# Decay exponents of an SSD mixer: from pairs of matmuls in PSUM to running sums that return broadcast from DRAM

## The reference, cut to what matters

```python
a_cs = jnp.cumsum(d * a, axis=2)                  # per chunk; d > 0, a < 0
seg = a_cs[:, :, :, None] - a_cs[:, :, None, :]   # l, s
decay = jnp.exp(jnp.where(causal, seg, -jnp.inf))
cb = jnp.einsum('bclgn,bcsgn->bclsg', cc, bc)
y_diag = jnp.einsum('bclsgr,bcsgrp->bclgrp', cb[..., None] * decay, xdt)
```

## Time and profile before

| | us |
|---|---|
| median of 3 runs (2773.5 to 2775.04) | 2773.87 |
| span of the profiled execution, first to last instruction | 2771.6 |
| TensorE busy | 2748.3 (99%) |
| VectorE busy | 1604.5 (58%) |
| ScalarE busy | 1183.0 (43%) |
| GpSimd busy | 1096.0 (40%) |
| DMA queue of SyncE, share of the 16 engines' span | 50.4% |

### The profile page before, as it was taken

How to read it: one execution, slowest core, us unless ns; L and a number is a source line. 1 busy time by engine, 2 the same in 40 slices (tenths; PEclk the granted TensorE clock), 3 DMA queues, 4 the chain that set the end, 5 groups by cost and what they waited for, 6 DMA issues and landing times.

```text
span 2771.6 us, 35692 instructions
## 1 busy us (share of the span) xinstructions
PE 2748.3 (99%) x13342; PEld 2298.7 (83%) x13342; DVE 1604.5 (58%) x2236; ACT 1183.0 (43%) x2110; POOL 1096.0 (40%) x799
## 2 busy tenths in 40 slices
PE   8999999999999999999999999999999999999998
PEld 6788888888888888888888888888888888888887
DVE  4687623666426665147673466664444666666666
ACT  2465544455325554155542545554454332222223
POOL 1365541223101222002233578866555435353434
PEclk9999999999999999999999999999999999999999
DMA  9765486443456335554436456584344942333323
GB/s 293 242 216 193 159 295 236 183 169 136 183 197 228 122 122 190 188 207 176 150 121 241 163 178 243 197 300 164 134 162 146 361 157 92 124 134 123 128 92 152
DMA packets 215786, 505.65 MB, mean 182 GB/s; under 512 B 12970, under 2 KB 96558, under 8 KB 206142
## 3 DMA queue, kind: packets, MB, share of 16 engines
q1 hardware_dynamic: 215614, 503.37, 50.4%
HBM read 357.57 MB, written 145.75 MB: 182 GB/s over the span
## 4 chain that ended last, share of the span: by engine, by line
PE 97%; DVE 1%; issue 1%; DMA 1%; POOL 0%; ACT 0%; DVEq 0%; POOLq 0%; ACTq 0%
PE bank L2024 22%; PE bank L1692 21%; PE bank L1992 21%; PE bank L1736 13%; PE bank L1716 7%; PE bank L1827 3%; PE bank L1832 2%; PE bank L1811 1%; PE bank L1633 1%; PE bank L1794 1%; PE bank L1783 1%; PE bank L1817 1%; PE bank L1805 1%; PE bank L1755 1%; PE bank L1947 0%
## 5 line engine op out<-in xcount | busy, mean ns | idle before, releaser
L1692 PE MATMUL bank<-hnT_hi,w_ring 128*128 128x512 f32 x1152 | 374.7, 396 | 0.0
L2161 DVE SCALAR_TENSOR_TENSOR acc<-pre,par,acc 128x512 f32<-128x512 f32 x240 | 217.1, 904 | 108.0 <-ACT pre L1230 102.3
L2024 PE MATMUL bank<-w_first,T_hi 128*128 128x512 f32 x896 | 275.9, 389 | 0.9 <-issue 0.9
L1692 PEld LDWEIGHTS bank<-hnT_hi,w_ring 128*128 128x128 f32 x1152 | 216.4, 188 | 44.9 <-ACT win_tmp L1339 0.5
L1992 PE MATMUL bank<-T_hi,w_both 128*128 128x512 f32 x768 | 242.1, 389 | 0.2 <-DVE ff L2444 0.2
L1736 PE MATMUL bank<-w_ring,T_hi 128*128 128x512 f32 x768 | 241.9, 396 | 0.0
L2503 DVE TENSOR_TENSOR acc_th<-bank,acc_th 128x512 f32<-128x512 f32 x224 | 149.9, 686 | 153.9 <-PE bank L2024 153.7
L983 POOL TENSOR_TENSOR small<-small 128x1 f32<-128x1 f32 (+1 forms) x71 | 17.9, 252 | 528.8 <-ACT yo L1313 322.3
L1692 PE MATMUL bank<-hnT_lo,w_ring 128*128 128x512 f32 x576 | 224.4, 390 | 0.0
L2024 PEld LDWEIGHTS bank<-w_first,T_hi 128*128 128x128 f32 x896 | 168.1, 188 | 36.0 <-issue 1.2
L1716 PE MATMUL bank<-w_ring,hnT_hi 128*128 128x384 f32 x768 | 197.9, 338 | 0.0
(11 more groups left out here) (310 smaller groups left out, 6339.7 us busy)
## 6 DMA issues: line engine op xcount, KB each, us to landing
w_ring<-w_scr SPq DMA_DIRECT2D x312, 512.0 KB, 4.2
T_scr<-stage SPq DMA_DIRECT2D x32, 1792.0 KB, 6.5
w_scr<-w_both SPq DMA_DIRECT2D x104, 512.0 KB, 4.0
pair_raw<-in_w_ff SPq DMA_DIRECT2D x36, 1024.0 KB, 5.4
third<-T_scr SPq DMA_DIRECT2D x28, 1024.0 KB, 4.8
pair_raw<-T_scr SPq DMA_DIRECT2D x28, 1024.0 KB, 4.8
raw<-in_w_in SPq DMA_DIRECT2D x36, 512.0 KB, 5.5
w_raw<-in_w_ff SPq DMA_DIRECT2D x12, 1024.0 KB, 7.4
```

Of the source, the lines that this page charges most:

```text
L1692: mm = nc.tensor.matmul(bank[s][:, :], w[:, k, :], t[:, k, :], start=(k == 0 and j == 0), stop=(k == KT - 1 and j == 2))
L2024: mm = nc.tensor.matmul(bank[4 * half + t][:, :], a[:, k, tok], w[:, k, :], start=(SECOND[q % 7] not in GOES_ON and k == 0 and j == 0), st ...
L2161: ins = nc.vector.scalar_tensor_tensor(acc[:, s, 0:TB], pre[:, s, k:k + TB], w, acc[:, s, 0:TB], ALU.mult, ALU.add)
```

## The change

E is now made without matmuls. The copy `acsT` (24 rows) is stored in DRAM once a block, in four small DMAs (`store_sums`), and each step's 768 sums (one chunk, six heads) come back by a DMA that reads the same 3 KB for all 128 partitions (`load_sums`, 384 KB a step), into one of four slots of `sums`, one for each chunk. ScalarE computes Relu(acs[s] - sums[l]) with six operations, one for each head, since the bias `acs` is one number per partition and head; then Exp(-x), in the first block too. `acs` gets a place of its own. The matmuls L1778 and L1783, `running_sums`, `negated_sums`, the low part and their set-up go; VectorE masks C x B in the first block too. The slots of group 0 are loaded right behind the stores, those of later groups one by one, each behind the Exp that read the slot before.

```diff
@@ block.sync
+                def store_sums(b):
+
+                    acsT_ready.wait(sp, b, 1)
+                    for g in range(GROUPS):
+                        rows = slice(g * HEADS_PER_GROUP, (g + 1) * HEADS_PER_GROUP)
+                        sp.dma_start(sums_scr[b, g].rearrange("c (r l) -> r c l", l=P),
+                                     acsT[rows, :].rearrange("r (c l) -> r c l", l=P)
+                                     ).then_inc(sums_stored.sem, 16)
+
+                def load_sums(b, g, c):
+
+                    if g:
+                        exp_ready.wait(sp, b, (g - 1) * CH + c + 1)
+                    sp.dma_start(sums[:, c, :, :].rearrange("p r l -> p (r l)"),
+                                 sums_scr[b, g, c].partition_broadcast(P)
+                                 ).then_inc(sums_loaded[c].sem, 16)
...
                     for n in range(RING, U_OUT):
                         load(N0 + n, in_unit(n))
+                        if n == 11:
+                            store_sums(b)
+                            sums_stored.wait(sp, b, 16 * GROUPS)
+                            for c in range(CH):
+                                load_sums(b, 0, c)
+                        g, j = divmod(n, UNITS_G)
+                        if g >= 2 or g == 1 and j >= 5:
+                            after = {5: 0, 7: 1, (0 if b else 1): 2, 3: 3}.get(j)
+                            done = g if j >= 5 else g - 1
+                            if after is not None and 0 < done < GROUPS:
+                                load_sums(b, done, after)
                         if n == 11 and b:
                             hT_ready.wait(sp, b - 1, KT)
@@ block.scalar
                         if q == 0:
                             acsT_ps.wait(act, b, 1)
-                            nc.scalar.activation(acsT[0:HEADS, :], bank[3][0:HEADS, :], ACT.Copy
-                                                 ).then_inc(acsT_hi_ready.sem, 1)
-                            negated_sums(b, 0)
+                            nc.scalar.activation(acsT, bank[3][0:HEADS, :], ACT.Copy
+                                                 ).then_inc(acsT_ready.sem, 1)
...
-                        ab_ps.wait(act, b, q + 1)
+                        sums_loaded[c].wait(act, b, 16 * (g + 1))
                         ydiag_ps.wait(act, b, q)
-                        halves = E[:, :, :].rearrange("p (j r) l -> p j (r l)", j=2)
-                        if b == 0:
-                            nc.scalar.activation(halves, decay_ps[:, :, 0:GW], ACT.Exp
-                                                 ).then_inc(exp_ready.sem, 1)
...
-                        if c == 0 and g + 1 < GROUPS:
-                            negated_sums(b, g + 1)
+                        for r in range(HEADS_PER_GROUP):
+                            o = c * HEADS + g * HEADS_PER_GROUP + r
+                            fall = nc.scalar.activation(E[:, r, :], sums[:, c, r, :], ACT.Relu,
+                                                        scale=-1.0, bias=acs[:, o:o + 1])
+                        fall.then_inc(fall_ready.sem, 1)
+                        fall_ready.wait(act, b, q + 1)
+                        nc.scalar.activation(E[:, :, :], E[:, :, :], ACT.Exp, scale=-1.0
+                                             ).then_inc(exp_ready.sem, 1)
@@ block.tensor, slot1
                     if q == 0:
                         down_add.wait(pe, b, 0)
-                    if g == 0:
-                        seg_l_ready.wait(pe, b, c + 1)
-                    if c == 0:
-                        seg_s_ready.wait(pe, b, g + 1)
-                    exponent_read(b, q)
-                    if b == 0:
-                        for j in range(2):
-                            nc.tensor.matmul(
-                                bank[4 + j][:, 0:GW].rearrange("p (r l) -> p r l", l=P),
-                                ident_r[:, :], barred[:, :].unsqueeze(1).to_broadcast([P, 3, P]),
-                                start=True, stop=False)
-                    for j in range(2):
-                        mm = nc.tensor.matmul(
-                            bank[4 + j][:, 0:GW].rearrange("p (r l) -> p r l", l=P),
-                            seg_s[:, g % 2, cols], seg_l[:, c, 3 * j:3 * j + 3, :],
-                            start=b > 0, stop=True)
-                    mm.then_inc(ab_ps.sem, 1)
+                        acsT_ready.wait(pe, b, 1)
@@ block.vector
                         cb = bank[3][:, GW:GW + P]
-                        if b:
-                            steps.link(nc.vector.tensor_tensor(cb, cb, tri[:, :], ALU.mult))
+                        steps.link(nc.vector.tensor_tensor(cb, cb, tri[:, :], ALU.mult))
...
-                        if q < CH - 1:
-                            running_sums(b, q + 1)
```

89 lines of the change are left out of this document (14 added, 75 removed).

## The result

The change made the kernel slower, by 12 us where 0.5 us of gain was forecast.

The account below looks back on a forecast made before the run. TensorE, busy 99% of the span, was taken as the bound. The terms -31.4 + 2.3 + 1 + 13.2 + 14.4 = -0.5 us on a span of 2771.6 gave a median of 2773.4 us, range 2756 to 2789.

Parts of the forecast that it names:

- ScalarE's lateness: Mixer steps where TensorE waits for a later ScalarE: 2.3 us lost in the first block, 1 us in later ones.
- What goes from TensorE: Exponent matmuls removed from all mixer steps: 12.2 us gained in the first block, 19.2 in later ones, together 31.4.
- 0.05 us a step for L1832: Each mixer step: L1832, then followed by a float32 transpose, takes 0.65 us instead of 0.70.
- Later blocks' gain: Later blocks lose L1783 alone: 0.40 us a step, 19.2 us gained over 48 steps.
- ScalarE: Each step: six Relus end after 1.85 us, where one took 0.86; bounds 1.6 and 2.4.
- First block's queue: First block's start: sums' transfers on SyncE delay the splits' stores, stalling units 10 to 12; 13.2 us, bounds 8 and 19.
- Later blocks' queue: Later blocks' starts: sums fill the DMA queue, unit 15's weights land late; 4.8 us a block, 14.4 in three.
- Rival 1: Later blocks: the queue hides the broadcasts, a block loses 0.5 us instead of 4.8; 2760 us, chance 0.27.
- Rival 2: Block starts: TensorE's clock falls to half in stalls from about 3 us on; 2783 us, chance 0.17.
- Rival 3: Relus or broadcasts at their upper bounds: 7 to 16 us more, 2785; chance 0.14 together with Rival 4.
- Rival 4: SyncE's waits for the Exps also stall steps; little effect expected, chance 0.14 together with Rival 3.

Follow-up runs that it names:

- the kernel without trips: The changed kernel without the sums' stores, broadcasts and waits through DRAM, their tile filled with zeros once: 2759.05 us, ratio 0.9947.
- the best order: The changed kernel with SyncE's transfers (sums, h) reordered and y's transposes of steps 0 to 13 in PSUM bank 4: 2753.96 us, ratio 0.9926.
- h later: The changed kernel with the 2 MB load of h behind the load of unit 20 instead of unit 12: 2780.0 us, ratio 1.0023.

## Why the prediction was wrong

The forecast was 28.1 us of gain (31.4 less 3.3 for ScalarE's lateness) against 27.6 of stalls. Measured by the kernel without trips: 14.6 against 26.8. **The step that failed is "What goes from TensorE": 31.4 us were put on the path, and taking the matmuls alone away gave 16.3.** That the loss came out within 1 us is luck, since two errors cancel in it: the first block's queue cost 6.8 us where 13.2 were forecast, the three later blocks 20.9 where 14.4 were. Step by step:

- **What goes from TensorE, 31.4 us.** This term failed. Its assumption was the sentence "TensorE is busy 99%: a matmul taken away is a gain as long as nothing new makes TensorE wait". An old wait could do it too: the one of 1.5 us for T_lo grew to 8.2 in six places without the trips. In the first block (12.2 us forecast, 9.9 with the lateness) the matmuls alone gave 3.70 us, and with the six Relus nothing was left of it. TensorE at a step's head must have T_lo, T_lo stands behind VectorE's taps, and VectorE was busy 4.9 to 5.0 of 5 us. What TensorE gained in the steps between it lost waiting there, and twice the gap opened far enough for the clock to fall. The prediction saw this for two of the last steps ("TensorE only comes earlier to wait", 1.3 us) and took it for a detail of the end. Of VectorE it said for the first block that "TensorE doesn't wait for it there"; its rows have VectorE's mean of 58% and no window of it in the mixer.
- **0.05 us a step for L1832.** Wrong: L1814 is still followed after 0.70 us (147.88 to 148.58), though float32 stands behind it. A step in the middle of a block gains 0.69 to 0.73 or 0.32 to 0.37, the pairs' own time. That is 3.2 of the 31.4.
- **Later blocks' gain.** 0.32 to 0.37 us a step up to step 11, but 0.16 to 0.20 in the last four: 14.3 us in three blocks (by the kernel without trips), where 19.2 less 1 was forecast. The last four are T_lo again: with y in another bank they gain 0.36.
- **ScalarE.** Six Relus take 1.85 to 1.87 us: the forecast to the hundredth. One instead of six gave 2.25 us, the forecast of the lateness was 3.3.
- **First block's queue.** Right in mechanism and time: split of unit 10 at 135.25 (134.3), unit 10 at 138.87 (138.0), unit 12 at 159.49 (160.0). From step 0 to step 2 12.5 us were lost, with 1.4 saved on the way 13.9 of stalls, forecast 13.2. But 4.9 of these are clock, not idle time, and TensorE's idle part is 9.0. Against the kernel without trips it costs only 6.8: the wait of 3.52 us for T_lo in step 2, and the half clock behind it and in step 12, which that kernel has, are not in the changed one. So the term was twice too large as a price, though right as a length of stalls.
- **Later blocks' queue.** 4.8 us a block were forecast. (Its 27 us for 9.9 MB are 2.7 us a MB, where 2.85 was named just before and would give 28.2; from the issue of the first broadcast at 514.73 to the landing of unit 15 at 544.1 it took 29.4, about 2 of it latency.) Lateness against the kernel without trips grew by 4.8 in the second block, by 8.2 and 7.9 in the third and fourth. The second block is the forecast (waits 0.95, 1.15 and 2.05). In the other two the same waits (2.25 and 2.28; 1.41 and 2.89) were followed by half speed: 0.66 granted from 910 to 915, and behind the shortest of them:

```profile
1258.00 1.52 PE L1809 MATMUL bank<-xdt,E 128*128 128x64 f32 x12 [1.41 <-issue]
...
1260.00:1265.00 5.00, 5.00 (x20) 3.95 (x19) 4.86 (x7) 2.66 (x8) 1.73 (x2) 0.69 0.98 398
```

- **Rival 1 (the queue hides it).** Refuted in every block.
- **Rival 2 (the clock falls), chance 0.17, 2783 us.** Near in time, and right that the clock falls; its point ("from a stall of about 3 us on") was too high, since stalls of 1.4 to 2.3 us were followed by it. That it explains the 12 us isn't shown: with the clock held at 1.00 the changed kernel took as long, and where it could be priced alone it was 2.2 us.
- **Rival 3 (Relus or broadcasts at their upper bounds).** Its 2785 is the nearest number, by luck: the Relus took 1.85 us, and the broadcasts flow as their plain size. In the full queue of the second block one (issued at 521.36) landed about 1.0 us behind the transfer before it, a plain one of 512 KB (519.83) about 1.3; and in the best order all 64 cost 1.4 us.
- **Rival 4 (SyncE's waits for the Exps).** None of TensorE's waits stands behind one.

The low end of the gain should have been open. A range of 28 to 31 for 80 pairs of matmuls was worked out from their durations alone; none of its bounds asked what stood idle beside them.

## What to carry to other kernels

A share of 99% says that an engine has no room, not that its every instruction is on the path: before a saving is counted at full price, read the busy time of its neighbours in the same windows. Where one of them is as full, and the engine waits for it now and then already, most of the saving can turn into that wait: 12.2 us by the sum were 3.7 here. When small transfers that others wait for are added to a queue, their place decides and not their bytes: the same 25 MB cost 26.8 us or, in another order and with y in its own bank, 1.4. And look at the bank space that a change sets free: with it the wait for T_lo was taken away, which gave 6.5 us, most of it in the first block, where the instructions themselves had given nothing.

## What the runs showed of the hardware

- In the changed kernel the granted clock fell to half behind the stalls of TensorE of 6.96, 2.89, 2.28, 2.25, 2.08 and 1.41 us, and not behind those of 2.15, 2.05 and 1.15 (315.86, 544.27, 533.56). In the kernel without trips it fell behind 3.52 and behind the same 2.15 us of T_lo (0.84 granted from 305 to 310). With h later, one of 2.40 us at 1257.99 was not followed by it. So between 1.4 and 2.4 us the length of the stall alone doesn't tell; what else decides isn't shown. That the runs of one kernel differ by 1 to 3 us may come from this, which wasn't tried.
- An operation of VectorE on 512 columns took 2.86 us beside one of 2.35 on GpSimd and 0.69 without it; three taps took 2.31, 3.52 or 5.47 us by what GpSimd did meanwhile. The Trainium skill, SBUF — State Buffer, SBUF: two separate sides, says that the two engines share a pair of ports as an exclusive lock, which a VectorE operation with two SBUF inputs needs against a GpSimd operation that reads SBUF. The rows agree: GpSimd began at 338.87, VectorE at 338.90, and VectorE ended 0.54 us after GpSimd. So moving TensorE by 0.7 us moved VectorE's taps by 2, through the time at which the split comes.
- Four stores of 12 KB, behind 3 MB in one queue, were known to have landed 8.5 us after their data was ready; in the first block, with little ahead of them, 2.5 us (121.98 to 124.49).
